# Level masks ahead of the inverse, keys times state ahead of the inverse: two edits to the gated DeltaNet of a two-layer encoder trunk

## The chip, the cores and the metric

One NeuronCore of a Trainium2 chip runs the whole program in one launch. The metric is the device time of one execution in microseconds (us). The engines are named as in the profile: PE (TensorE matmuls), PEld (its weight loads, which overlap PE), DVE (VectorE), ACT (ScalarE), POOL (GpSimd) and SP (SyncE, which issues most DMAs). PE's clock is granted at one of two levels, 1.2 and 2.4 GHz; a granted clock of 1.00 is the upper one, 0.50 the lower one.

## What is computed

The input is 512 tokens of 1024 channels, float32. Each of two layers is a half-step SwiGLU feed-forward, a token mixer, and another half-step feed-forward. In the mixer a combined projection feeds a gated DeltaNet branch (4 heads of 128) and a sliding-window attention branch. The part that the change touches is the gated delta rule:

```python
lower = jnp.where(strict, jnp.einsum('bnhid,bnhjd->bnhij', k_beta, kc) * decay, 0.0)
a_mat = jnp.eye(CHUNK) + lower
rhs = jnp.concatenate([v_beta, k_beta * jnp.exp(gc)[..., None]], axis=-1)
sol = triangular_solve(a_mat, rhs, left_side=True, lower=True, unit_diagonal=True)
u_c, w_c = sol[..., :dv], sol[..., dv:]
def step(state, inp):
    v_new = u_i - w_i @ state
    o = (q_i * exp(g_i)) @ state + a_i @ v_new
    state = state * exp(g_last) + (k_i * exp(g_last - g_i)).T @ v_new
```

So new values are A⁻¹ V − (A⁻¹ K) S, with A unit lower triangular, S the running state of a head and K the keys scaled by their decay.

## The kernel before, in words

PE's time goes into weight matmuls. Weights come from HBM in chunks of 128x1024; each is loaded by a DMA of SP into one of two raw buffers, copied by ACT to a rounded high part (line 911, `whi`), and the rest is made by DVE (line 1295, `wlo`): that pair is called the split of a chunk. PE multiplies each tile three times (lines 522 to 524: high by high, high by low, low by high). In the mixer, chunk j's 24 matmuls of 512 columns (12 for the half-size chunks 16 to 19) are followed by the list `MIX_STEPS[j]`, which is written out by hand in `mix_steps`. All five engines walk the same list in the same order, each doing its own part of every step; each engine is strictly in order, and the split of chunk j+3 is the first thing that ACT and DVE do in step list j. The steps hand PSUM banks 4 to 7 (and 2, 3) to each other through two counters per bank: `misc[b]` (PE has written it) and `misc_out[b]` (it has been read). `banks_of` says which bank a step uses; `count_uses` numbers the uses.

The steps that matter here, in the order of the list:

- `ktr` t: PE transposes the keys of token tile t; ACT squares them (line 1100, for the norm), DVE scales them twice, to `kte` (line 1584) and `ktl` (line 1585). `knorm` and `kk` then make the masked product matrix `NN`.
- SP takes the 16x16 diagonal blocks of `NN` out through HBM (`dg_home`, `tri`). `solve` (lines 1547 to 1557): DVE inverts them by a chain of 30 small, linked instructions. SP sends the result round through HBM again to `blk`, and `zb` (lines 1535 and 1542) makes from it Z, two halves of eight 64x64 inverses, and its transpose `Zt`.
- `invp` and `invd` i, lev: for each half i, two levels (4: 16 to 32, 5: 32 to 64) of doubling the inverted blocks. `invp` multiplies `Zt` by `Cs`, the part of `NN` that the level's mask keeps. `Cs` is made by POOL (line 1768) in the step itself, after POOL has seen both halves of Z; PE's part is line 721. ACT copies the product to `Pm` (line 1127), and `invd` (PE line 733, DVE line 1571) multiplies and subtracts. All of these are 64x64 matmuls of 32 columns.
- `vx`, `zx`, `zcp` complete the 128x128 inverse `Zf` from the halves.
- `wt` t (chunks 25 and 26): PE multiplies `kte` by `Zf` (line 779), ACT copies minus the product to `wneg` (line 1176).
- `sv` t (chunk 25+3t): PE accumulates `Zf` times values `vtm` (line 823) and, for t over 0, `wneg` times state S (line 825); DVE scales to `vn` (line 1621).
- `so` t (chunk 26+3t): PE makes the output and the state's update (lines 833, 841, 846), DVE makes S (lines 1628, 1633) and `o`.
- `vtr` t: transposes of the values (PE line 742, ACT line 1121). `qtr` t: transposes of the queries into bank 5 (PE line 698), squared by ACT (line 1111). `vwin`: transposes of the attention's values into bank 5, copied by ACT (lines 1167, 1168). `rope`, `swap`, `kmask` (ACT line 1149, which waits for the fifth `rope`): rotary positions. `sc`, `scn`, `pt`, `pv`: the windowed attention.

## Time and profile before

| | us |
|---|---|
| median of 3 runs | 2246.32 |
| lowest, highest of them | 2243.83, 2246.43 |
| profiled execution, its own time | 2241.95 |
| its span, first to last instruction | 2240.2 |
| PE busy in the span | 2212.7 (99%) |
| DVE, ACT, POOL busy | 1005.5, 845.0, 76.0 |
| mean granted clock of PE | 0.997 |

Times in the profile are counted from the span's start. The first mixer lies at about 390 to 760 us, the second at about 1500 to 1870 us. PE rows overlap (a matmul's row runs on while the next has begun), so what a group of matmuls costs is read from its start to the start of the next group. A float32 matmul is recorded as two rows, so the 16 matmuls of 128x128 in two `wt` steps and the like show twice their number.

### The profile page before, as it was taken

The numbers are of one execution on the slowest core, as the hardware profiler recorded it, in microseconds if no ns is written. First come the engines' busy times: TensorE is split into PE (matmuls) and PEld (weight loads), VectorE is DVE, ScalarE is ACT, GpSimd is POOL, SyncE is SP. The second block draws the span as 40 slices with busy tenths as digits, with TensorE's granted clock in tenths as the row PEclk, the third lists the DMA queues.
The fourth block names the chain that finished last, engine by engine and source line by source line (L and its number), as shares of the span: only waits on it lengthen the run. The fifth ranks groups of instructions, "written<-read, shape, count | busy, mean of one in ns | idle before, by whom it ended". The sixth has DMA issues, their size and how long they took to land. (4 is left out here: it accounts for less than half of the span.)

```text
span 2240.2 us, 29019 instructions
## 1 busy us (share of the span) xinstructions
PE 2212.7 (99%) x11356; PEld 1855.9 (83%) x11356; DVE 1005.5 (45%) x1422; ACT 845.0 (38%) x1499; POOL 76.0 (3%) x104
## 2 busy tenths in 40 slices
PE   7999999999999999999999999999999999999998
PEld 7888888888888888888888888887788888888887
DVE  4434324595536543442253433246944456344323
ACT  5323214655533532331252322156555335223211
POOL 0000000001000100000000000010100001000000
PEclk9999999999999999999999999999999999999999
DMA  4232222332123333222232232223312242332232
GB/s 164 94 99 96 96 97 82 124 91 67 57 76 124 107 107 99 97 94 96 84 113 94 94 103 94 95 84 123 92 57 66 84 142 89 101 102 94 94 100 79
DMA packets 71126, 215.83 MB, mean 96 GB/s; under 512 B 18928, under 2 KB 19440, under 8 KB 70256
## 3 DMA queue, kind: packets, MB, share of 16 engines
q1 hardware_dynamic: 69008, 201.82, 27.7%
q0 software_dynamic: 2016, 12.58, 1.5%
q8 instruction: 72, 1.18, 0.2%
q14 instruction: 30, 0.25, 0.0%
HBM read 206.77 MB, written 7.60 MB: 96 GB/s over the span
## 5 line engine op out<-in xcount | busy, mean ns | idle before, releaser
L1295 DVE TENSOR_TENSOR wlo<-raw,whi 128x1024 fp32r<-128x1024 f32 (+1 forms) x376 | 457.9, 1218 | 895.8 <-ACT whi L911 885.8
L522 PE MATMUL ps<-uhi,whi 128*128 128x512 f32 (+1 forms) x2208 | 829.8, 376 | 3.7 <-DVE wlo L1295 1.6
L523 PE MATMUL ps<-ulo,whi 128*128 128x512 f32 (+1 forms) x2208 | 821.5, 372 | 0.0
L524 PE MATMUL ps<-uhi,wlo 128*128 128x512 f32 (+1 forms) x2208 | 821.3, 372 | 0.0
L911 ACT ACTIVATE whi<-raw 128x1024 fp32r<-128x1024 f32 (+1 forms) x372 | 390.9, 1051 | 930.7 <-PE ps L524 547.2
L522 PEld LDWEIGHTS ps<-uhi,whi 128*128 128x128 f32 x2208 | 418.5, 190 | 78.3 <-issue 4.2
L524 PEld LDWEIGHTS ps<-uhi,wlo 128*128 128x128 f32 x2208 | 418.1, 189 | 72.2
L523 PEld LDWEIGHTS ps<-ulo,whi 128*128 128x128 f32 x2208 | 418.4, 189 | 69.8
L569 PE MATMUL ps<-whi,hhi 128*128 128x512 f32 x704 | 274.4, 390 | 0.0
L571 PE MATMUL ps<-whi,hlo 128*128 128x512 f32 x704 | 274.0, 389 | 0.0
L570 PE MATMUL ps<-wlo,hhi 128*128 128x512 f32 x704 | 273.9, 389 | 0.0
L571 PEld LDWEIGHTS ps<-whi,hlo 128*128 128x128 f32 x704 | 132.1, 188 | 27.6
L570 PEld LDWEIGHTS ps<-wlo,hhi 128*128 128x128 f32 x704 | 132.2, 188 | 27.2
L569 PEld LDWEIGHTS ps<-whi,hhi 128*128 128x128 f32 x704 | 132.2, 188 | 27.2
L998 ACT ACTIVATE tmp<-ps 128x512 f32<-128x512 f32 x88 | 52.8, 600 | 98.9 <-PE ps L524 98.4
L1376 DVE SCALAR_TENSOR_TENSOR tmp<-tmp,ps 128x512 f32<-128x512 f32 x88 | 60.2, 684 | 41.8 <-ACT tmp L998 41.8
L1001 ACT ACTIVATE hhi<-tmp 128x512 f32 (+1 forms) x88 | 55.5, 630 | 51.4 <-DVE tmp L1379 51.4
L1715 POOL TENSOR_TENSOR ry<-msy,neghalf 128x1 f32<-128x1 f32 x24 | 17.9, 744 | 1494.2 <-DVE msy L1302 1494.2
L1385 DVE SCALAR_TENSOR_TENSOR hlo<-tmp,hhi 128x512 f32 (+1 forms) x88 | 60.6, 689 | 12.0 <-ACT hhi L1001 10.8
L1379 DVE TENSOR_TENSOR tmp<-tmp,ps 128x512 f32<-128x512 f32 x88 | 60.5, 688 | 7.7
L1479 DVE SCALAR_TENSOR_TENSOR tmp<-cv,prm,tmp 128x512 f32<-128x512 f32 x72 | 54.0, 750 | 7.9 <-ACT tmp L1062 6.1
L1337 DVE SCALAR_TENSOR_TENSOR ulo<-ps,prm,uhi 128x256 fp32r<-128x256 f32 x96 | 42.2, 480 | 30.4 <-ACT uhi L961 30.4
(216 smaller groups left out, 1573.6 us busy)
## 6 DMA issues: line engine op xcount, KB each, us to landing
raw<-in_wstream_dram SPq DMA_DIRECT2D x368, 512.0 KB, 3.4
x_home<-x POOLq DMA_DIRECT2D x4, 1024.0 KB, 4.3
x<-x_home POOLq DMA_DIRECT2D x2, 2048.0 KB, 8.5
gain<-in_gp_dram POOLq DMA_DIRECT2D x6, 512.0 KB, 6.0
x<-in_x_dram SPq DMA_DIRECT2D x4, 512.0 KB, 7.8
raw<-in_wstream_dram SPq DMA_DIRECT2D x8, 256.0 KB, 3.7
out_dram<-x SPq DMA_DIRECT2D x8, 256.0 KB, 2.0
rcs<-in_rope_dram POOLq DMA_DIRECT2D x2, 512.0 KB, 4.1
```

Of the source, the lines that this page charges most:

```text
L522: pe.matmul(o, lh, bhi, start=first, stop=False)
L523: pe.matmul(o, lh, blo, start=False, stop=False)
L524: return pe.matmul(o, ll, bhi, start=False, stop=last)
L569: pe.matmul(o, shi[:, k, tok], whi[:, s, w], start=k == 0, stop=False)
L570: pe.matmul(o, shi[:, k, tok], wlo[:, s, w], start=False, stop=False)
L571: last = pe.matmul(o, slo[:, k, tok], whi[:, s, w], start=False, stop=k == kn - 1)
L911: act.activation(whi[:, s, 0:cols], raw[:, s % RAWS, 0:cols], ACT.Copy).then_inc(hi_done.h, 1)
L1001: act.activation(hhi[:, bass.ds(it * 2 + i, 1), :].rearrange("p a s -> p (a s)") if not isinstance(it, int) else hhi[:, 2 * it + i, :], tm ...
L1295: dve.tensor_tensor(wlo[:, s, 0:cols], raw[:, s % RAWS, 0:cols], whi[:, s, 0:cols].bitcast(f32), ALU.subtract) \
L1376: dve.scalar_tensor_tensor(tmp[:, i, :], tmp[:, 4 + i, :], 1.0, bank(4 * odd + 2 * i), ALU.add, ALU.mult).then_inc(tile_read.h, 1)
L1379: dve.tensor_tensor(tmp[:, 2 + i, :], tmp[:, i, :], bank(4 * odd + 2 * i + 1), ALU.mult).then_inc(tile_read.h, 1)
L1385: dve.scalar_tensor_tensor(lo, tmp[:, 2 + i, :], 0.5, hi.bitcast(f32), ALU.mult, ALU.subtract) \
```

## The change

It has four parts. (1) The masks `Cs` of level 4 are made by POOL in a new step `cmask` of list 14, as soon as DVE has finished `silu` 10, which is the instruction ahead of its `solve`; those of level 5 stay where they were. The two halves of `zb` are made one after the other (multiply, transpose, multiply, transpose). (2) `wt`, `kte` and `wneg` are gone. For t over 0 a new step `ks` in list 24+3t multiplies the keys by the state S ahead of the inverse, DVE scales it by the decay and subtracts the values from it into `vtm`, and `sv` has only the product by `Zf`, whose sign DVE turns while it scales. (3) The steps around the inverse are reordered: `vtr` 3 between the two `invp` of level 4, `qtr` 2 between the two `invd` of level 5, `qtr` 3 ahead of the evacuations of list 23, and `kmask` behind `vwin` 0 and `qtr` 0. (4) `qtr` squares into other buffers, which are free one `rope` earlier.

```diff
@@ mix_steps
-    s[14] = [("conv", 11), ("silu", 10), ("solve",)]
+    s[14] = [("conv", 11), ("silu", 10), ("solve",), ("cmask",)]
...
-    s[18] = [("qk", 0), ("qk", 1), ("rope", 2), ("rope", 3), ("vtr", 3)]
-    s[19] = [("evac", 16), ("evac", 17), ("swap", 4), ("invp", 0, 4), ("invp", 1, 4), ("rope", 4)]
-    s[20] = [("kmask",), ("vwin", 0), ("invd", 0, 4), ("qtr", 0), ("invd", 1, 4)]
+    s[18] = [("qk", 0), ("qk", 1), ("rope", 2), ("rope", 3)]
+    s[19] = [("evac", 16), ("evac", 17), ("swap", 4), ("invp", 0, 4), ("vtr", 3), ("invp", 1, 4), ("rope", 4)]
+    s[20] = [("vwin", 0), ("invd", 0, 4), ("qtr", 0), ("kmask",), ("invd", 1, 4)]
...
-    s[22].insert(0, ("qtr", 2))
-    s[23].insert(4, ("qtr", 3))
+    s[22].insert(1, ("qtr", 2))
+    s[23].insert(0, ("qtr", 3))
     s[24] = [("zx", 0), ("zx", 1), ("lq",)]
-    s[25] = [("qk", 3), ("wt", 0), ("wt", 1)]
-    s[26] = [("wt", 2), ("wt", 3)]
+    s[25] = [("qk", 3)]
+    s[26] = []
...
     for t in range(TT):
+        if t:
+            s[24 + 3 * t].append(("ks", t))
         s[25 + 3 * t].append(("sv", t))
@@ PE
-                    elif k == "wt":
-                        ...
-                            last = pe.matmul(bank(b, h * P, P), kte[:, t, h, :], Zf[:, 4 * t + h, :], start=True, stop=True)
+                    elif k == "ks":
+                        t = step[1]
+                        use(L, step, 4)
+                        pe.wait_ge(s_new.h, s_new.at(L, t))
+                        free_of_waits()
+                        for h in range(H):
+                            last = pe.matmul(bank(4, h * P, P), kq[:, 0, h, P * t:P * t + P], S[:, h, :], start=True, stop=True)
+                        done(last, 4)
...
                         if t:
-                            got(("wt", t), banks_of(("wt", t))[0])
-                            pe.wait_ge(s_new.h, s_new.at(L, t))
+                            got(("ks", t), 4)
...
                         for h in range(H):
-                            last = pe.matmul(bank(4, h * P, P), Zf[:, 4 * t + h, :], vtm[:, t, h, :], start=True, stop=t == 0)
-                            if t:
-                                last = pe.matmul(bank(4, h * P, P), wneg[:, h, P * t:P * t + P], S[:, h, :], start=False, stop=True)
+                            last = pe.matmul(bank(4, h * P, P), Zf[:, 4 * t + h, :], vtm[:, t, h, :], start=True, stop=True)
@@ ACT
                         if t == 0:
-                            act.wait_ge(roped.h, roped.at(L, 5))
+                            act.wait_ge(roped.h, roped.at(L, 4))
...
-                            last = act.activation(tmp[:, 2 + t % 2, h * P:(h + 1) * P], bank(5, h * P, P), ACT.Square,
+                            last = act.activation(tmp[:, 4 + t % 2, h * P:(h + 1) * P], bank(5, h * P, P), ACT.Square,
...
-                    elif k == "wt":
-                        ...
@@ DVE
-                        for i in range(2):
-                            s8 = slice(8 * i, 8 * i + 8)
                             dve.wait_ge(z1_done.h, z1_done.at(L, i + 1))
                             dve.transpose(Zt[:, s8, :].rearrange("p c j -> p (c j)"), Z[:, s8, :].rearrange("p c j -> p (c j)")) \
...
-                        dve.tensor_tensor(kte[:, t, :, :], src, cols(exs, 4 * t, 4, P), ALU.mult)
...
-                        dve.tensor_tensor(vn[:, :, :], bank(4).rearrange("p (h d) -> p h d", d=P), cols(wcol, 4 * t, 4, P), ALU.mult) \
+                        dve.scalar_tensor_tensor(vn[:, :, :], bank(4).rearrange("p (h d) -> p h d", d=P), -1.0 if t else 1.0,
+                                                 cols(wcol, 4 * t, 4, P), ALU.mult, ALU.mult).then_inc(misc_out[4].h, 1)
+                    elif k == "ks":
+                        t = step[1]
+                        ready(step, 4)
+                        got(("vtr", t), banks_of(("vtr", t))[0])
+                        for h in range(H):
+                            last = dve.scalar_tensor_tensor(vtm[:, t, h, :], bank(4, h * P, P), exs[:, 4 * t + h:4 * t + h + 1], vtm[:, t, h, :],
+                                                            ALU.mult, ALU.subtract)
+                        last.then_inc(misc_out[4].h, 1)
@@ POOL
+                def level_mask(i, lev):
+                    s8 = slice(8 * i, 8 * i + 8)
+                    pool.tensor_tensor(Cs[:, s8, :], NN[:, s8, 0:CH], many(con[:, K_LEV + 64 * (lev - LEVELS[0]):][:, 0:64], 8),
+                                       ALU.mult).then_inc(c_done.h, 1)
...
+                    elif k == "cmask":
+                        pool.wait_ge(silu_done.h, silu_done.at(L, 11))
+                        for i in range(2):
+                            level_mask(i, LEVELS[0])
...
-                        pool.tensor_tensor(Cs[:, s8, :], NN[:, s8, 0:CH], many(con[:, K_LEV + 64 * (lev - LEVELS[0]):][:, 0:64], 8),
-                                           ALU.mult).then_inc(c_done.h, 1)
-                        if lev > LEVELS[0]:
+                            level_mask(i, lev)
```

## Rows read from the trace of the kernel before

**Rows 1.** Page, part 1: busy us, share, instructions of each engine.
```profile
PE 2212.7 (99%) x11356; PEld 1855.9 (83%) x11356; DVE 1005.5 (45%) x1422; ACT 845.0 (38%) x1499; POOL 76.0 (3%) x104
```

**Rows 2.** Waits of PE: us in total, times, longest.
```profile
PE ps L698 <- ACT vwin L1168: 3.5, 2, 2.6
...
PE ps L721 <- issue: 0.9, 2, 0.6
```

**Rows 3.** Timeline of PE, chunks 25 and 26: start, us, idle before.
```profile
562.20 1.95 PE L779 MATMUL ps<-Zf,kte 128*128 128x128 f32 x16
564.08 0.66 PE L809 MATMUL ps<-pT,vwin 64*64 64x128 f32 x8
...
566.03 1.05 PE L823 MATMUL ps<-vtm,Zf 128*128 128x128 f32 x8
566.84 0.48 PE L522 MATMUL ps<-uhi,whi 128*128 128x512 f32 x1
```

**Rows 4.** Timeline of PE, `sv` 1 of the first mixer.
```profile
593.22 0.38 PE L823 MATMUL ps<-vtm,Zf 128*128 128x128 f32 x2
...
594.92 0.48 PE L522 MATMUL ps<-uhi,whi 128*128 128x512 f32 x1
```

**Rows 5.** Groups by line, DVE.
```profile
L1584 DVE TENSOR_TENSOR kte<-ps,exs 128x512 f32<-128x512 f32 x8 | 5.5, 684 | 0.0
```

**Rows 6.** Timeline of DVE around the end of list 27.
```profile
587.09 0.15 DVE L1648 SCALAR_TENSOR_TENSOR mo<-sso,eqs 128x4 f32<-128x4 f32 x1
...
605.94 1.12 DVE L1633 SCALAR_TENSOR_TENSOR S<-S,exs,ps 128x128 f32<-128x128 f32 x4 [1.25 <-PE ps L846]
```

**Rows 7.** Timeline of PE, second mixer, list 20.
```profile
1624.63 0.66 PE L698 MATMUL ps<-con,kq 128*128 128x128 f32 x4 [2.57 <-ACT vwin L1168]
```

**Rows 8.** Timeline of PE, first mixer, chunk 18 and list 19.
```profile
494.67 0.48 PE L522 MATMUL ps<-uhi,whi 128*128 128x512 f32 x1
...
503.18 1.12 PE L721 MATMUL ps<-Zt,Cs 64*64 64x32 f32 x32 [0.53 <-POOL Cs L1768]
504.87 1.12 PE L721 MATMUL ps<-Zt,Cs 64*64 64x32 f32 x32 [0.57 <-issue]
506.31 0.52 PE L522 MATMUL ps<-uhi,whi 128*128 128x512 f32 x1 [0.32 <-ACT sk L1055]
```

**Rows 9.** Timeline of POOL and DVE, first mixer, list 19.
```profile
503.51 1.26 POOL L1768 TENSOR_TENSOR Cs<-NN,con 128x512 f32<-128x512 f32 x1
...
503.74 2.12 DVE L1295 TENSOR_TENSOR wlo<-raw,whi 128x1024 fp32r<-128x1024 f32 x1 [0.81 <-ACT whi L911]
```

**Rows 10.** Timeline of DVE, first mixer: the solve and what follows.
```profile
486.39 0.17 DVE L1551 TENSOR_TENSOR prod<-tri,sol 128x15 f32<-128x15 f32 x1
...
493.50 0.69 DVE L1295 TENSOR_TENSOR wlo<-raw,whi 128x512 fp32r<-128x512 f32 x1
...
499.28 1.23 DVE L1295 TENSOR_TENSOR wlo<-raw,whi 128x1024 fp32r<-128x1024 f32 x1
500.42 1.29 DVE L1535 TENSOR_TENSOR Z<-blk,con 128x512 f32<-128x512 f32 x2
501.62 1.30 DVE L1542 STREAM_TRANSPOSE Zt<-Z 128x512 f32<-128x512 f32 x2
```

**Rows 11.** Second mixer: DVE's split of chunk 18, PE's start on it.
```profile
1602.18 0.69 DVE L1295 TENSOR_TENSOR wlo<-raw,whi 128x512 fp32r<-128x512 f32 x1
...
1604.07 0.48 PE L522 MATMUL ps<-uhi,whi 128*128 128x512 f32 x1
```

**Rows 12.** Windows: us, busy (x) of PE, PEld, DVE, ACT, POOL, granted clock, DMA.
```profile
506.00:510.00 4.00, 3.69 (x9) 2.94 (x10) 3.97 (x7) 3.07 (x7) 1.00 (x1) 0.57 0.40 133
533.00:538.00 5.00, 5.00 (x104) 4.79 (x103) 1.23 (x4) 1.14 (x8) 0.00 (x0) 0.93 0.35 108
538.00:541.00 3.00, 3.00 (x10) 2.48 (x10) 1.17 (x5) 1.38 (x10) 0.95 (x1) 0.55 0.00 0
...
1626.00:1629.00 3.00, 3.00 (x18) 2.40 (x15) 2.36 (x3) 1.53 (x5) 0.53 (x1) 0.53 0.18 72
```

More of the change, by code:

```diff
@@ L161, in banks_of @@
         return ((7, 4) if x == 0 else (6, 7))[:1 if step[2] == LEVELS[0] else 2]
-    if k == "wt":
-        return (7,) if x % 2 == 0 else (4,)
     if k == "pt":
@@ L261, in trunk @@
         kq = at("kq", [P, 2, H, SEQ], 0)
-        wneg = at("wneg", [P, H, SEQ], 0)
         vT = at("vT", [P, H, SEQ], 16 * kb)
@@ L280, in trunk @@
         Zt = at("Zt", [P, 16, CH], 68 * kb)
-        kte = at("kte", [P, TT, H, P], 72 * kb)
         cv = at("cv", [P, 4, 516], 80 * kb)
@@ L1172, in do @@
                                            ACT.Copy).then_inc(misc_out[5].h, 1)
-                    elif k == "wt":
-                        t, b = step[1], banks_of(step)[0]
-                        ready(step, b)
-                        act.activation(wneg[:, :, t * P:(t + 1) * P], bank(b).rearrange("p (h c) -> p h c", c=P), ACT.Copy,
-                                       scale=-1.0).then_inc(misc_out[b].h, 1)
                     elif k == "sc":
@@ L1538, in do @@
                                .then_inc(z1_done.h, 1)
-                        for i in range(2):
-                            s8 = slice(8 * i, 8 * i + 8)
                             dve.wait_ge(z1_done.h, z1_done.at(L, i + 1))
```

14 lines of the change are left out of this document (5 added, 9 removed).

## The prediction, as it was put on record before the run

> **What bounds the kernel now.** I read the page first. PE is busy 99% of the span and DVE and ACT under half [rows 1], so a change is worth what it does to PE's line of work: matmuls taken off it, and waits of PE that end or begin. Shorter work elsewhere counts only where PE waits for it. So the second view is PE's own waits. In the mixers they are few: 3.5 us in two waits of `qtr` 0 for ACT's copy of `vwin` (line 1168), and about 1.4 us of `invp` (line 721) for POOL's masks, 0.9 put down to "issue" [rows 2] and 0.5 to POOL [rows 8]. The third is the timeline of PE and DVE through lists 14 to 26, where the change lies, and the fourth the granted clock in windows there, because the timeline shows chunks that run slow behind the small matmuls.
>
> **`wt` gone.** From the start of `wt` 0 to the start of what follows it is 564.08 - 562.20 = 1.88 us for two steps [rows 3]. There are two such pairs in a mixer and two mixers: 4 x 1.88 = 7.5 us of PE's time, with nothing beside it.  ACT's four copies to `wneg` go too, and were hidden.
>
> **`sv` and `ks`.** `sv` 1 with both products takes 594.92 - 593.22 = 1.70 us [rows 4]. After, `sv` is like `sv` 0, 566.84 - 566.03 = 0.81 us [rows 3], and `ks` has the same four matmuls, 0.81 to 0.9. The sum is the same as before. What is added is one more place where PE changes from weight matmuls to a step, six times; the first matmul behind a step is longer than the others (0.48 us in [rows 3]), so I allow 0.07 us each, an estimate, +0.4 us in all (bounds 0 and +0.6).
>
> **Does PE wait for `ks`?** `ks` t needs S from the list before, and `sv` t needs DVE's result one chunk after `ks`. DVE's part is four scalar_tensor_tensor of 128x128 from PSUM, which is the form of line 1633: 1.12 us for four [rows 6]. In front of it in DVE's queue are the softmax's four small instructions and `on`, whose end is at 587.24 [rows 6]. So DVE is done near 588.5, and PE asks for it at about 593.2, when `sv` 1 stood before [rows 4]. The cover is over 4 us; the cost is 0. What queues behind DVE's wait in that list is `zsilu` and the split of chunk 31, three chunks ahead of PE; both wait for ACT anyway. If that cover were gone, every microsecond of lateness would cost six.
>
> **`kmask` behind `qtr`.** In list 20 ACT waits for the fifth `rope` before it may copy `vwin` 0, and PE stands behind bank 5: 2.57 us in the second mixer, the rest of the 3.5 in the first [rows 2, 7]. After, ACT reads bank 5 as soon as PE has written it, and PE has `invd` 0 in between, 32 small matmuls like those of line 721, 1.12 us [rows 8], longer than ACT's copy. DVE's own lateness there is met by a chunk of cover before `invp` of level 5. I take all of it: -3.5 us (bounds -3.5 and -2.5, if DVE's later `zt` should reach PE).
>
> **Masks early: the gain and its price.** The gain is bounded by the 1.4 us [rows 2, 8]. In the first mixer `invp` 0 starts at 503.18 after 0.53 us and `invp` 1 after 0.57 [rows 8]; `Zt` is the next to be late, and it was there at 502.9 at the latest [rows 10].
>
> The price is in the place where the masks go. `cmask` is released by the same instruction of DVE behind which `solve` begins, at 486.39 [rows 10], and POOL reaches for the memory together with a chain of 30 linked DVE instructions. The trace shows what POOL's mask does to a DVE instruction that reads two SBUF tensors: the split that starts at 503.74, with POOL's `Cs` running from 503.51 to 504.77, takes 2.12 us [rows 9], and the one at 499.28, of the same shape, 1.23 [rows 10]. That is a hold until POOL's instruction has ended. No row shows it for the solve's small ones, so I bound: the hold is between 0 and 2 x 1.26 = 2.5 us a mixer, and I take 2.5, by the nearest row. From it goes what DVE no longer does: 4 x 0.6 us for `kte` (0.684 as recorded, 0.6 from start to start) [rows 5]. Of these 2.4 us about half is lost again, since the second `ktl` must wait for ACT's squares; I follow DVE's continuous row of work from `ktr` to `kk` 3 and get 1.15 us. So the solve ends about 2.5 - 1.15 = 1.35 us later (bounds -1.15 and +2.5).
>
> What is late next: the first thing behind the solve is the split of chunk 18, done at 494.19 where PE starts on chunk 18 at 494.67 [rows 8, 10]: only 0.48 us of cover, less 0.1 for the handover, so PE waits about 0.95 us. In the second mixer the cover is 1604.07 - 1602.87 = 1.20 [rows 11], and PE waits 0.25. The result's two DMAs, `zb`, the next load and ACT's evacuations behind it all move by the same 1.35. `invp` 0 then finds `Zt` at about the time it comes, and chunk 20 waits for ACT's evacuation of `sk`, as it did before by 0.32 [rows 8], now some 0.65 later, as ACT no longer has `vtr` 3 in front. Chunk 20 starts at about 507.0 for 506.31, and 0.6 late in the second mixer. So the masks' gain and price together are +1.2 us; with no hold they are -1.4, with the full hold and nothing from `kte` +3.7.
>
> The Trainium skill's page "GPSIMD Engine Reference" (section "Key points") says that POOL shares its SBUF interfaces with VectorE and contends with DVE instructions that have two SBUF inputs; by it the solve, all of whose instructions have two, is held as the split was, and the sum is the one I take; were the rule not to reach them, the sum would be that of the second rival. The rule speaks against this change, and the row of the split agrees with it, 2.12 us for 1.23.
>
> **The clock.** Three stretches of the mixers ran at half the clock: 0.57 over 506 to 510, 0.55 over 538 to 541 with 0.93 before it [rows 12], and 0.53 over 1626 to 1629 [rows 12]. Each costs (1 - 0.57) x 4 = 1.7 us, or (1 - 0.55) x 3 + (1 - 0.93) x 5 = 1.7. Before each, PE had 3 to 4 us of nothing but 64x64 matmuls of 32 columns and waits. Two of the three had a wait in them that the change ends or shortens, and the third was two `invd` and their double products back to back (104 matmul rows in 533 to 538). After, `vtr` 3, `qtr` 0 and `qtr` 2 (128x128, 128 columns) stand between them. The second mixer has no fall at the place of the third, so it is not certain even before. I take 2.4 of the three falls as gone: -4.0 us (bounds 0 and -5.1). An early stall of 0.9 us at chunk 18 does not stand beside small matmuls.
>
> **The rest.** `qtr` 3 ahead of the evacuations delays ACT by 1.8 us into list 24; I find `zx` still covered by 0.4 us or more. `vn` as scalar_tensor_tensor reads and writes the same elements, and DVE is far from the bound there. Both 0.
>
> **Sum.** -7.5 + 0.4 - 3.5 + 1.2 - 4.0 = -13.4 us. On the profiled execution that is 2241.95 - 13.4 = 2228.5, its span 2226.8. The three timed runs stand 1.9 to 4.5 us above that execution, for no reason that the profile shows; I carry the difference over to the median: 2246.3 - 13.4 = 2232.9 us, -0.6%.
>
> **Rivals.**
> - *The full hold and a clock that still falls.* POOL's masks cost 2.5 us a mixer with no relief, and the new stall and the still small matmuls keep the falls: -7.5 + 0.6 - 3.5 + 3.7 = -6.7, 2239.6 us. For it: the cover of 0.48 us. Against: the waits inside the small stretches do shrink. 0.2.
> - *No hold.* The solve's instructions slip between POOL's, the masks' waits are gone: -7.5 - 3.5 - 1.4 - 5.1 = -17.5, 2228.8 us. For it: no row of a small instruction held. Against: the row of the split. 0.2.
> - *Nothing is left.* The freed PE time turns into waits for something else, the weights' loads first: within 4.5 us of before. For it only that the chunks 16 to 20 are already near their loads; against, the rest of the mixer has splits three chunks ahead. 0.05.
> - *Slower: `ks` is not covered.* If DVE's part of `ks` came after `sv`'s place, PE would stand six times. To end 4.5 us over before, it has to eat 13.4 + 4.5 = 17.9 us, 3.0 us each: DVE would have to end 7 us later than the 588.5 above, behind the next splits. That gives 2251 us. Its point of decision is the end of DVE's fourth instruction against PE's `sv`. 0.03.
>
> **How the numbers follow.** The forecast has 0.5 (its own range 2230 to 2236, from the 1.2 and the 4.0 each going half-way to their bounds), the rivals 0.48, and 0.02 is for more than all of it. 0.2% of 2246 is 4.5 us, about what a measurement of this kernel can tell from no change. The range of 8 in 10 reaches from the second rival to the first and takes in a spread of the runs of about 1.5 us on the lower side: 2227 to 2240. Faster 0.91, same 0.05, slower 0.04.
>
> **What would show it.** No rows of lines 779 and 1176, a `ks` line with 48 rows on PE, `sv` with 64. POOL's `Cs` of level 4 inside the solve, with two instructions of lines 1551 and 1553 of over 1 us instead of 0.2: the hold. PE idle before chunk 18 of the first mixer for about 1 us behind `wlo`, less in the second. No wait of `qtr` behind `vwin`. `sv` without a wait for `vtm`. Windows of half clock in the mixers: none or one for three. The prediction is wrong if the solve ends more than 2.5 us later, if PE waits at `zx` or `sv`, or if the clock falls as often as before.

## The result, and the profile after

The changed kernel takes 2229.73 us (median of 5, 2228.74 to 2229.96). The kernel before has a median of 2243.83 over five runs (2239.06 to 2246.43), of which three are those of the table above and two are new. The ratio is 0.9941, 95% interval 0.9929 to 0.9953: 0.6% faster. The profiled execution took 2229.16, its span 2227.4, which is 12.8 us less than the span before.

The page's part 1 shows PE 12.9 us less busy than in [rows 1], with 64 rows fewer, which are the 32 matmuls of `wt`, each recorded as two rows.

```profile
PE 2199.8 (99%) x11292; PEld 1842.5 (83%) x11292; DVE 1013.8 (46%) x1438; ACT 841.5 (38%) x1491; POOL 74.7 (3%) x104
```

PE's waits after the change, to be read against [rows 2] (us in total, times, longest):

```profile
PE ps L783 <- DVE attnT L1519: 2.6, 2, 1.3
...
PE ps L520 <- ACT sk L1050: 1.7, 2, 0.8
...
PE ps L719 <- DVE Zt L1530: 0.5, 2, 0.3
```

The 3.5 us of `qtr` behind `vwin` are gone. New, and not forecast, is `sc` 3 (line 783) behind `attnT`, DVE's multiply of `qk` 3: 1.3 us in each mixer.

DVE's timeline where the solve begins in the first mixer, and the split of chunk 18 behind it, against [rows 10]:

```profile
483.73 0.17 DVE L1539 TENSOR_TENSOR prod<-tri,sol 128x15 f32<-128x15 f32 x1
483.94 1.29 DVE L1541 TENSOR_TENSOR sol<-sol,prod 128x15 f32<-128x15 f32 x1
485.26 1.22 DVE L1539 TENSOR_TENSOR prod<-tri,sol 128x28 f32<-128x28 f32 x1
486.51 0.19 DVE L1541 TENSOR_TENSOR sol<-sol,prod 128x28 f32<-128x28 f32 x1
...
492.97 0.69 DVE L1285 TENSOR_TENSOR wlo<-raw,whi 128x512 fp32r<-128x512 f32 x1
```

And POOL's timeline at the same place:

```profile
483.89 2.54 POOL L1738 TENSOR_TENSOR Cs<-NN,con 128x512 f32<-128x512 f32 x2 [26.91 <-DVE kq L1482]
```

Two instructions of the solve take 1.29 and 1.22 us while POOL makes its two masks, where 0.17 to 0.20 is usual: a hold of 1.1 + 1.05 = 2.15 us. Measured from PE's first transpose of v, at 490.68 before and 489.65 after, the solve starts 1.63 us sooner, and the split of chunk 18 comes 0.50 later. The second mixer shows the change alone: there the solve starts 1.01 us sooner (at 1595.07 with the transpose at 1600.08 before, at 1586.73 with 1592.75 after), and the split of chunk 18 comes 1.14 later than in [rows 11]. About 0.5 of the first mixer's 1.63 is no part of the change: `order_alone` and `masks_alone` (below), which still have `kte`, start the solve 0.49 and 0.44 us sooner than before there, and within 0.1 us of before in the second mixer. In the trace of before, ACT's split ahead of the solve waited 2.64 us for a late load, and DVE stood 0.87 us for ACT. The two rows are ACT's of before and DVE's of the changed kernel:

```profile
482.26 0.64 ACT L911 ACTIVATE whi<-raw 128x512 fp32r<-128x512 f32 x1 [2.64 <-DMA raw<-in_wstream_dram]
```
```profile
1595.99 0.69 DVE L1285 TENSOR_TENSOR wlo<-raw,whi 128x512 fp32r<-128x512 f32 x1
```

PE's timeline at chunk 18, list 19, `qtr` 0 and list 25 of the first mixer, against [rows 3, 8]:

```profile
493.71 0.50 PE L520 MATMUL ps<-uhi,whi 128*128 128x512 f32 x1
...
501.50 1.12 PE L719 MATMUL ps<-Zt,Cs 64*64 64x32 f32 x32 [0.26 <-DVE Zt L1530]
...
505.08 0.47 PE L520 MATMUL ps<-uhi,whi 128*128 128x512 f32 x1 [0.81 <-ACT sk L1050]
...
512.23 0.66 PE L696 MATMUL ps<-con,kq 128*128 128x128 f32 x4
...
557.68 0.66 PE L794 MATMUL ps<-con,pexp 128*128 128x128 f32 x4
559.67 1.10 PE L783 MATMUL ps<-skz,sq 128*128 128x256 f32 x4 [1.33 <-DVE attnT L1519]
560.61 1.05 PE L820 MATMUL ps<-vtm,Zf 128*128 128x128 f32 x8
```

No row of PE shows a wait at chunk 18, but the split ends only 0.05 us ahead of it in the first mixer (493.66 for 493.71) and 0.06 in the second (1596.68 for 1596.74). `qtr` 0 starts without idle time. `sc` 3 is what PE now waits for.

The clock, in windows from the first transpose of v to `vx` in each mixer, the stretch in which the windows of [rows 12] lie:

```profile
489.65:540.29 50.64, 49.57 (x490) 41.70 (x488) 36.74 (x64) 26.74 (x76) 5.76 (x7) 1.00 0.30 90
1592.75:1643.34 50.59, 49.50 (x489) 41.69 (x488) 36.76 (x63) 26.75 (x76) 5.71 (x7) 1.00 0.30 90
```

The granted clock is 1.00 in both: none of the three falls to the 1.2 GHz level is left. This is no accident of one execution: the mean granted clock over the whole span is on record for every timed run, and it is 0.999 in all five of the changed kernel and all five of `changed_again` (below), while 42 of the 44 timed runs of before that have one lie between 0.995 and 0.998 (one has 0.993, one 0.999).

To compare the kernels, PE's line of work is cut at the same steps in each. Stretch A goes from the first v transpose to `vx`, stretch B from `vx` to the first transpose of `o`. The rest of the two mixers is equal to 0.1 us in all kernels (except in `qk3_late`, told below). The clock is the mean granted clock in A. All times are from the profiled execution of each; the last columns are timed runs.

| kernel | A, mixer 1 (clock) | A, mixer 2 (clock) | B, mixers 1, 2 | span | median (low to high) | ratio to before, interval |
|---|---|---|---|---|---|---|
| before | 54.75 (0.94) | 53.94 (0.97) | 57.09, 57.09 | 2240.2 | 2243.83 (2239.06 to 2246.43) | |
| changed | 50.64 (1.00) | 50.59 (1.00) | 55.00, 55.00 | 2227.4 | 2229.73 (2228.74 to 2229.96) | 0.9941, 0.9929 to 0.9953 |
| `changed_again` | 50.69 (1.00) | 50.58 (1.00) | 54.98, 54.99 | 2227.7 | 2230.03 (2229.48 to 2231.62) | 0.9951, 0.9938 to 0.9965 |
| `keys_alone` | 53.06 (0.97) | 55.98 (0.91) | 53.69, 53.69 | 2233.2 | 2235.28 (2232.73 to 2237.39) | 0.9973, 0.9962 to 0.9985 |
| `order_alone` | 50.05 (1.00) | 49.74 (1.00) | 57.04, 57.04 | 2229.9 | 2232.72 (2231.64 to 2235.61) | 0.9965, 0.9951 to 0.9978 |
| `masks_alone` | 54.84 (0.94) | 54.88 (0.94) | 57.08, 57.08 | 2240.0 | 2244.47 (2241.33 to 2248.94) | 1.0016, 1.0007 to 1.0025 |
| `qk3_late` | 52.34 (0.97) | 50.45 (1.00) | 52.58, 52.58 | 2225.5 | 2227.3 (2226.3 to 2228.0) | 0.9935, 0.9922 to 0.9949 |
| `qtr3_back` | 50.64 (1.00) | 50.55 (1.00) | 53.70, 53.71 | 2224.7 | 2228.24 (2226.48 to 2228.63) | 0.9941, 0.9927 to 0.9955 |
| `masks_back` | 49.33 (1.00) | 49.33 (1.00) | 54.98, 54.98 | 2224.5 | 2226.81 (2226.25 to 2228.08) | 0.9937, 0.9923 to 0.9950 |
| `masks_twice` | 52.55 (1.00) | 52.78 (1.00) | 54.99, 54.98 | 2231.6 | 2234.26 (2233.38 to 2236.15) | 0.9970, 0.9957 to 0.9982 |
| `kmask_back` | 56.27 (0.94) | 58.49 (0.91) | 53.70, 53.73 | 2238.3 | 2239.43 (2237.27 to 2241.73) | 0.9990, 0.9981 to 0.9998 |
| `slices_back` | 56.08 (0.94) | 52.68 (0.97) | 53.72, 53.71 | 2232.3 | 2231.84 (2229.48 to 2234.07) | 0.9954, 0.9940 to 0.9969 |
| `masks_13` | 51.73 (0.97) | 50.05 (1.00) | 55.01, 54.99 | 2227.7 | 2228.69 (2228.25 to 2229.91) | 0.9943, 0.9929 to 0.9956 |
| `both_back` | 49.33 (1.00) | 49.33 (1.00) | 53.72, 53.69 | 2221.9 | 2224.14 (2223.2 to 2224.5) | 0.9922, 0.9908 to 0.9935 |

`changed_again` is the changed kernel once more, on the chip of the kernels that it is compared with. Three sets shared a chip and the runs of before: `keys_alone`, `order_alone`, `masks_alone`, `qk3_late` (before 2240.95); `changed_again`, `qtr3_back`, `masks_back`, `masks_twice` (before 2241.76); and `kmask_back`, `slices_back`, `masks_13`, `both_back` (before 2241.34).

### The profile page after: what moved, and what is told of

The parts are those of the page before. It is cut to its first block and busy times, and to the rows that moved or that the text cites. A ratio compares the mean times of both kernels' runs of the same rounds, so it can differ in the third digit from the quotient of the medians.

```text
span 2227.4 us, 28889 instructions
## 1 busy us (share of the span) xinstructions
PE 2199.8 (99%) x11292; PEld 1842.5 (83%) x11292; DVE 1013.8 (46%) x1438; ACT 841.5 (38%) x1491; POOL 74.7 (3%) x104
```

## The experiments

**One part of the change at a time.** Three kernels are the kernel before with one part of the change each. `keys_alone`:

```diff
-    s[25] = [("qk", 3), ("wt", 0), ("wt", 1)]
-    s[26] = [("wt", 2), ("wt", 3)]
+    s[25] = [("qk", 3)]
+    s[26] = []
+        if t:
+            s[24 + 3 * t].append(("ks", t))
...
-                        dve.tensor_tensor(kte[:, t, :, :], src, cols(exs, 4 * t, 4, P), ALU.mult)
```

> The kernel before with ks in the place of wt and without kte and wneg; masks, v slice 3, the q squares' place and kmask as before. Theory from the two traces: the 64 matmuls of wt (7.5 us) go, but the 1.88 us of wt 0 and wt 1 had hidden what sc 3 waits for (bank 5, which DVE's multiply of qk 3 frees), so a wait of about 1.3 us a mixer stands in front of sc 3 (2.6), and the sum is -4.7 with the clock unchanged: about 2239 against 2244. kte's relief of DVE (0.6 a mixer) reaches a little of the stalls at chunks 18 to 20, -0.5 at most. Rival 1, nothing is exposed: -7.1. Rival 2, what the removal does to the clock: each fall of the clock inside a mixer that is gone gives 1.6 to 1.7 more, each new one takes as much, and the windows with a granted clock under 0.9 show which.

Measured: 0.9973, 5.7 us under before. B is 3.40 shorter in each mixer, 6.8 in all: `wt`'s 7.5 less 0.7, which I put down to the `ks` and `sv` steps standing apart (it is the remainder, not a row). The expected wait of `sc` 3 is not there; nothing stands between `pt` 1 and `sc` 3 but `pt`'s own 0.64 us, and PE's timeline has no idle time before it:

```profile
560.77 0.66 PE L794 MATMUL ps<-con,pexp 128*128 128x128 f32 x4
561.41 1.10 PE L783 MATMUL ps<-skz,sq 128*128 128x256 f32 x4
```

So the removal of `wt` alone does not expose the wait; the theory I had from the two traces was wrong. ACT's timeline of this kernel in list 23 shows what differs. It evacuates z at once and squares `qtr` 3 (line 1106) behind that:

```profile
541.29 2.31 ACT L1050 ACTIVATE z<-ps 128x512 f32<-128x512 f32 x4
543.50 0.27 ACT L1106 ACTIVATE tmp<-ps 128x128 f32<-128x128 f32 x1
```

In the changed kernel ACT comes to `qtr` 3 first and stands 2.02 us until PE has made the transposes:

```profile
540.39 0.28 ACT L1106 ACTIVATE tmp<-ps 128x128 f32<-128x128 f32 x1 [2.02 <-PE ps L696]
...
541.66 2.07 ACT L1050 ACTIVATE z<-ps 128x512 f32<-128x512 f32 x4
```

DVE's multiply of `qk` 3 follows from it. In `keys_alone` it starts 1.38 us behind PE's `qk` 3, which PE began at 559.20, and in the changed kernel 2.73 us behind it, begun at 556.11. The two rows of DVE, `keys_alone` first:

```profile
560.58 0.68 DVE L1519 TENSOR_TENSOR attnT<-attnT,ps 128x512 f32<-128x512 f32 x1
```
```profile
558.84 0.68 DVE L1519 TENSOR_TENSOR attnT<-attnT,ps 128x512 f32<-128x512 f32 x1
```

The clock moved as well: 0.97 and 0.91 for 0.94 and 0.97. The falls cost (1 - 0.97) x 53.06 + (1 - 0.91) x 55.98 = 6.6 us, where those of before cost (1 - 0.94) x 54.75 + (1 - 0.97) x 53.94 = 4.9. And this kernel, which makes the masks where before made them, has no wait of `invp` for them in either mixer: with `kte` gone they are there in time.

`order_alone` (its list edits; with them `qtr`'s squares go to `tmp` 4 and 5 and wait for four `rope`s in place of five):

```diff
-    s[18] = [("qk", 0), ("qk", 1), ("rope", 2), ("rope", 3), ("vtr", 3)]
-    s[19] = [("evac", 16), ("evac", 17), ("swap", 4), ("invp", 0, 4), ("invp", 1, 4), ("rope", 4)]
-    s[20] = [("kmask",), ("vwin", 0), ("invd", 0, 4), ("qtr", 0), ("invd", 1, 4)]
+    s[18] = [("qk", 0), ("qk", 1), ("rope", 2), ("rope", 3)]
+    s[19] = [("evac", 16), ("evac", 17), ("swap", 4), ("invp", 0, 4), ("vtr", 3), ("invp", 1, 4), ("rope", 4)]
+    s[20] = [("vwin", 0), ("invd", 0, 4), ("qtr", 0), ("kmask",), ("invd", 1, 4)]
-    s[22].insert(0, ("qtr", 2))
-    s[23].insert(4, ("qtr", 3))
+    s[22].insert(1, ("qtr", 2))
+    s[23].insert(0, ("qtr", 3))
```

> The kernel before with the reordering alone: v slice 3 between invp 0 and invp 1, kmask behind q square 0, the squares' scratch tiles, q squares 2 and 3 each a step earlier; wt, kte and masks as before. Theory from the two traces: the wait of q square 0 behind vwin's copy goes (3.5 us over both mixers), and nothing else is lost: -3.5. If the falls of the clock come from the small matmuls that stand together at chunks 18 to 20 and 22 to 24, they are gone here too and the time is 5 lower still, -8.5; if wt was the cause of a fall, they stay and it is -3.5. Rival: invp 0 comes 0.6 us sooner and waits for its masks and for Zt that much longer (0.6 a mixer, 1.2), which leaves -2.3.

Measured: 0.9965, 8.2 us under before. A is 4.69 and 4.20 shorter, 8.9 in all, and the windows show a full clock:

```profile
489.61:539.67 50.06, 49.51 (x490) 41.71 (x488) 35.83 (x60) 26.71 (x76) 8.57 (x9) 1.00 0.29 91
1594.13:1643.87 49.74, 49.48 (x489) 41.70 (x487) 35.62 (x59) 26.74 (x76) 8.55 (x9) 1.00 0.31 91
```

Of the 8.9, the falls were 4.9 and the waits 4.0. So the reordering can take all three falls away without `wt` or the masks being touched. (The profiled execution, 2231.64, is the fastest of this kernel's five. The slowest, 2235.61, has a mean clock of 0.999 over its span like the profiled one; two falls more would show in that number, so falls do not account for the 4.0 us between them.) `invp` still waits 0.9 us in all for POOL's masks, so `vtr` 3 between the two `invp` does not end that wait by itself. Here PE still has `wt` 0 and 1 (1.88 us) between `qk` 3 and `sc` 3, and B is unchanged: ACT's lateness is covered by them.

`masks_alone` (`cmask` beside the solve, `zb`'s halves one after the other, all else as before):

```diff
-    s[14] = [("conv", 11), ("silu", 10), ("solve",)]
+    s[14] = [("conv", 11), ("silu", 10), ("solve",), ("cmask",)]
```

> The kernel before with the masks alone: the level 4 masks on POOL while DVE runs the substitution, and zb's two halves each with its transpose. Theory: POOL's two masks hold DVE by about 1.1 us each (2.15 a mixer), the solve ends 2.15 later than before (there is no relief of kte here), the split of chunk 18 is that late and PE stands at chunk 18 for 1 to 2 us; the waits for Cs (0.53 a mixer) go, part of the lateness falls into chunk 20's own waits. Sum +1 to +3 over both mixers. Rival 1, PE has enough in front of it that the hold is paid by nobody: -0.5 to -1.4. Rival 2, the clock: a stall longer than before moves a fall, +-1.7 each.

Measured: 1.0016, 3.5 us over before, a little more than expected. The profiled execution is not the place to read it: at 2241.80 it lies at the low end of runs from 2241.33 to 2248.94, and its span is that of before. It does show the kind: the waits of PE at chunks' starts grow (wlo 3.7 us for 1.6, sk 3.3 for 0.6), while the 3.5 of `qtr` 0 behind `vwin` is gone. That PE has lost that time earlier fits both, but was not tested.

```profile
PE ps L522 <- DVE wlo L1295: 3.7, 8, 1.0
PE ps L522 <- ACT sk L1055: 3.3, 2, 1.7
```

**Where the wait of `sc` 3 comes from.** `qk3_late` is the changed kernel with the step that holds bank 5 taken away from there:

```diff
-    s[25] = [("qk", 3)]
+    s[25] = []
+    s[30].append(("qk", 3))
```

> The changed kernel with qk 3 taken out of list 25 and put at the end of list 30, where bank 5 has been read for the last time and so 3 (list 35) is still five chunks away. Theory: sc 3 waits in the changed kernel for bank 5, which DVE's multiply of qk 3 frees (1.3 us a mixer), so this gives 2.6 us over the changed kernel: about 2227, and the wait row of sc 3 behind DVE attnT is gone. Rival: sc 3 then waits for the exponentials of sc 2 or for another of DVE's jobs of the same stretch, and the wait only changes its name: within 0.5 us of the changed kernel. Second rival: the multiply, now in list 30, holds a step of the state chain there: slower by up to 1.3 in place of faster.

Measured: 0.9935. Against `changed_again` B is 2.40 shorter in each mixer, and the stretch up to the last transpose of `o`, which now holds `qk` 3, is 1.02 longer in the first mixer and 0.90 in the second: 1.4 and 1.5 us net, for the 1.3 expected. The row of `sc` 3 behind `attnT` is gone. It gives 2.9 in the trace, of which a fall of the clock in the first mixer (0.97) takes back 1.6. The cause of the wait was then tested at the other end, in `qtr3_back`, the changed kernel with one number changed:

```diff
-    s[23].insert(0, ("qtr", 3))
+    s[23].insert(4, ("qtr", 3))
```

> The changed kernel with q square 3 back behind the four evacuations of list 23, where it stood before; all else as changed. Theory: in the changed kernel ACT reaches the squares of q square 3 first, waits there 2.02 us for PE's transposes and evacuates only then, so its split of chunk 28, and with it DVE's multiply of qk 3, come 1.4 us later against PE than with the keys alone; so the wait of sc 3 (1.3 us a mixer) comes from this move and goes with it: 2.6 under the changed kernel, and no wait row of sc 3 behind DVE attnT. Rival 1: PE has moved ahead of the whole DVE queue by the 3.5 us that the reordering gave it, whatever ACT does, and the wait stays: within 0.5 of the changed kernel. Rival 2: vx waits for the later evacuations, which takes it back.

Measured: B is 1.28 shorter in each mixer, 2.6 in all, A and the clock are unchanged, and the wait is gone. ACT evacuates 3.3 us sooner than in the changed kernel, and PE goes from `pt` 1 to `sc` 3 without a stop:

```profile
538.36 2.31 ACT L1050 ACTIVATE z<-ps 128x512 f32<-128x512 f32 x4
```
```profile
557.84 0.66 PE L794 MATMUL ps<-con,pexp 128*128 128x128 f32 x4
558.47 1.10 PE L783 MATMUL ps<-skz,sq 128*128 128x256 f32 x4
```

By the timed runs it is 1.8 us under `changed_again`, on medians with ranges of 2.1 us each. So the chain is: PE's `qtr` 3, ACT's wait of 2.0, ACT's later split, DVE's later multiply of `qk` 3, bank 5, `sc` 3. PE itself makes the same steps in the same order in both kernels.

**What the masks cost.** `masks_back` is the changed kernel with level 4's masks in `invp` and `zb` as before:

```diff
-    s[14] = [("conv", 11), ("silu", 10), ("solve",), ("cmask",)]
+    s[14] = [("conv", 11), ("silu", 10), ("solve",)]
```

> The changed kernel with the masks as before (level 4 in invp, both of zb's products ahead of the transposes); keys and reordering as changed. Theory: the reordering alone against the changed kernel puts the masks at +0.6 and +0.85 us from the first v transpose to vx, so without them it is 1.4 under the changed kernel: about 2228.3; DVE's substitution runs from its start to its end in 9.3 less 2.15 us, and a wait for Cs of about 0.6 stands at invp 0 again. Rival 1: the wait for Cs is worth as much as the hold: within 0.5. Rival 2: without the stall at chunk 20 or with the one at invp 0 a fall of the clock comes back: 1.7 slower for each.

Measured: 0.9937, 3.2 us under `changed_again` on the same chip. A is 1.36 and 1.25 shorter: 2.6 us, about twice what I expected. PE is busy for all of the 49.33 us of A in both mixers: no wait for `Cs`, for `Zt` or for `sk` is left. DVE's timeline has the solve from 483.45 to the split at 490.55, 7.10 us, where the changed kernel takes 9.24:

```profile
483.45 0.17 DVE L1541 TENSOR_TENSOR prod<-tri,sol 128x15 f32<-128x15 f32 x1
...
490.55 0.68 DVE L1285 TENSOR_TENSOR wlo<-raw,whi 128x512 fp32r<-128x512 f32 x1
```
```profile
489.45:538.78 49.33, 49.33 (x490) 41.64 (x488) 33.72 (x55) 26.67 (x76) 9.02 (x9) 1.00 0.31 92
```

`masks_twice` doubles the suspected cost:

```diff
                         for i in range(2):
+                            pool.tensor_tensor(Cs[:, 8 * i:8 * i + 8, :], NN[:, 8 * i:8 * i + 8, 0:CH],
+                                               many(con[:, K_LEV:][:, 0:64], 8), ALU.mult).then_inc(pool_link.h, 1)
+                            pool.wait_ge(pool_link.h, pool_link.at(L, 2 + i))
                             level_mask(i, LEVELS[0])
```

> The changed kernel with each of the two level 4 masks made twice by POOL, one product behind the other, so that POOL runs four products of 1.27 us beside the substitution in place of two. Theory: while POOL's product runs, DVE's instruction does not end, so four instructions of the substitution take 1.2 to 1.3 us in place of 0.2, the solve ends 2.15 later than in the changed kernel, and since DVE has next to nothing to spare up to chunk 18, PE pays 1.5 to 2.1 of it in each mixer: +3 to +4.3 against the changed kernel. Rival 1: the hold is a single one at the start of POOL's work, not one for each product: below +0.5. Rival 2: the hold is there, but waits that stand there anyway (0.8 at chunk 20, 0.26 at invp 0) take it up: +1 to +2.

Measured: 4.2 us over `changed_again`, A longer by 1.86 and 2.20. Four instructions of POOL, four long ones of DVE; each is held until POOL's has ended. POOL's and DVE's timelines:

```profile
484.07 1.30 POOL L1762 TENSOR_TENSOR Cs<-NN,con 128x512 f32<-128x512 f32 x1 [26.84 <-DVE kq L1482]
485.45 1.34 POOL L1738 TENSOR_TENSOR Cs<-NN,con 128x512 f32<-128x512 f32 x1
```
```profile
484.11 1.30 DVE L1541 TENSOR_TENSOR sol<-sol,prod 128x15 f32<-128x15 f32 x1
485.45 0.19 DVE L1539 TENSOR_TENSOR prod<-tri,sol 128x28 f32<-128x28 f32 x1
485.67 1.17 DVE L1541 TENSOR_TENSOR sol<-sol,prod 128x28 f32<-128x28 f32 x1
486.88 1.23 DVE L1539 TENSOR_TENSOR prod<-tri,sol 128x39 f32<-128x39 f32 x1
488.14 1.35 DVE L1541 TENSOR_TENSOR sol<-sol,prod 128x39 f32<-128x39 f32 x1
```

The wait of PE for `wlo` grows from 1.6 to 5.4 us, which is the price at the chunk behind the solve. PE stands 1.9 us there in each mixer, behind the 512-column matmuls of a chunk and one step of transposes, and the granted clock of A stays at 1.00.

Which instructions of DVE are held can be read from before's own masks, which run beside others. After the split of [rows 9] DVE's next two rows, whose inputs are one tile in SBUF and one in PSUM (`ps`), take 0.65 us each beside POOL's second mask, no more than the 0.68 of one elsewhere. POOL's row, which starts while the split still runs, takes 1.80 in place of 1.28:

```profile
505.20 1.80 POOL L1768 TENSOR_TENSOR Cs<-NN,con 128x512 f32<-128x512 f32 x1
```
```profile
505.88 1.29 DVE L1529 TENSOR_TENSOR attnT<-attnT,ps 128x512 f32<-128x512 f32 x2
```
 `masks_13` moves the masks beside longer instructions with two inputs in SBUF:

```diff
-    s[13] = [("conv", 10), ("silu", 9)]
-    s[14] = [("conv", 11), ("silu", 10), ("solve",), ("cmask",)]
+    s[13] = [("cmask",), ("conv", 10), ("silu", 9)]
+    s[14] = [("conv", 11), ("silu", 10), ("solve",)]
```

> The changed kernel with POOL's two level 4 masks moved from the substitution to list 13, beside DVE's convolution, where DVE's instructions are 0.7 to 0.8 us long and DVE has 0.61 and 0.25 us of idle time before the solve. Theory: POOL's product holds DVE wherever DVE works, long instructions as well (2.15 us in all), but 0.86 of it falls into the idle time there: the solve starts 1.3 later and takes 2.15 less, 0.4 to 0.9 a mixer under the changed kernel, 0.8 to 1.7 in both. Rival 1: long instructions are not held, and it is worth the whole of masks_back, 2.6 under. Rival 2: the idle time there is not real slack, since ACT's chain moves with DVE: within 0.4 of the changed kernel.

Measured: 0.9943, as good as the changed kernel. In the second mixer A is 0.53 shorter than in `changed_again`, as expected; in the first it is 1.04 longer, with a clock of 0.97, which is (1 - 0.97) x 51.73 = 1.6 us, so 0.5 shorter but for the fall. The hold has moved with the masks, to a split and to the convolution's three instructions together, 1.37 for 0.69 and 3.36 for 2.33:

```profile
476.33 1.37 DVE L1285 TENSOR_TENSOR wlo<-raw,whi 128x512 fp32r<-128x512 f32 x1 [0.57 <-ACT whi L906]
477.62 3.36 DVE L1469 SCALAR_TENSOR_TENSOR tmp<-cv,prm,tmp 128x512 f32<-128x512 f32 x3
```

**What brings the clock down.** Two kernels undo one part of the reordering each, and are read against `qtr3_back`. `kmask_back`:

```diff
-    s[20] = [("vwin", 0), ("invd", 0, 4), ("qtr", 0), ("kmask",), ("invd", 1, 4)]
+    s[20] = [("kmask",), ("vwin", 0), ("invd", 0, 4), ("qtr", 0), ("invd", 1, 4)]
-    s[23].insert(0, ("qtr", 3))
+    s[23].insert(4, ("qtr", 3))
-                            act.wait_ge(roped.h, roped.at(L, 4))
+                            act.wait_ge(roped.h, roped.at(L, 5))
```

> The changed kernel with q square 3 behind the evacuations (as in qtr3_back, the comparison for this one) and kmask back at the head of list 20, with the squares' scratch tiles and their wait for roped as before; v slice 3 and q square 2 stay where the change put them. Theory: ACT's copy of vwin 0 comes behind kmask again and PE stands at q square 0 for 1.75 to 2.6 us a mixer: +3.5 to +5.1 over qtr3_back. On the clock, theory A: PE's standing still there is what brings the falls inside the mixers, so one to three come back at 1.7 each: +5 to +10 in all. Theory B: it is the small matmuls that stand together in front of chunks 20 and 22, which this kernel still has spread: no fall, +3.5 to +5.1.

Measured: A longer by 5.63 and 7.94 us, 13.6 in all, more than either theory allowed; the timed median is 11.2 higher (on another chip). PE's waits and the windows:

```profile
PE ps L696 <- ACT vwin L1163: 6.3, 2, 3.2
```
```profile
489.77:546.04 56.27, 52.08 (x490) 43.61 (x488) 36.90 (x64) 28.53 (x80) 5.82 (x7) 0.94 0.26 81
1597.12:1655.61 58.49, 54.26 (x490) 45.41 (x488) 36.58 (x64) 28.63 (x80) 5.93 (x7) 0.91 0.27 83
```

The wait is 6.3 us, where before had 3.5 and `keys_alone` 5.1; DVE's `rope` behind the held solve may be what makes it longer, which no run here tests. The falls cost (1 - 0.94) x 56.27 + (1 - 0.91) x 58.49 = 8.6. The two together are 14.9, against 13.6: the two overlap in part, and where PE stands anyway a fall costs nothing. Not all of the falls belong to the wait. One in the second mixer begins at the end of list 22, where `qtr` 2 stands between the small matmuls as in the changed kernel and PE has no wait:

```profile
1642.00:1647.00 5.00, 5.00 (x99) 4.36 (x98) 0.81 (x3) 1.14 (x8) 0.00 (x0) 1.00 0.30 105
1647.00:1650.50 3.50, 3.50 (x18) 3.05 (x18) 1.66 (x6) 0.64 (x5) 0.95 (x1) 0.54 0.02 5
```

`slices_back`:

```diff
-    s[18] = [("qk", 0), ("qk", 1), ("rope", 2), ("rope", 3)]
-    s[19] = [("evac", 16), ("evac", 17), ("swap", 4), ("invp", 0, 4), ("vtr", 3), ("invp", 1, 4), ("rope", 4)]
+    s[18] = [("qk", 0), ("qk", 1), ("rope", 2), ("rope", 3), ("vtr", 3)]
+    s[19] = [("evac", 16), ("evac", 17), ("swap", 4), ("invp", 0, 4), ("invp", 1, 4), ("rope", 4)]
-    s[22].insert(1, ("qtr", 2))
-    s[23].insert(0, ("qtr", 3))
+    s[22].insert(0, ("qtr", 2))
+    s[23].insert(4, ("qtr", 3))
```

> The changed kernel with q square 3 behind the evacuations (as in qtr3_back, the comparison for this one), v slice 3 back in list 18 and q square 2 back at the head of list 22; kmask stays behind q square 0. No work is added and no wait is known of. Theory A on the clock (the wait at q square 0 brings the falls): no fall inside a mixer, within 0.6 of qtr3_back in the trace; invp 0 and invp 1 run without the 0.58 of v slice 3 between them, so a wait for the second half's Zt of up to 0.7 a mixer can show: +0 to +1.4. Theory B (small matmuls standing together): one to three falls come back at 1.7 each: +1.7 to +5.

Measured: median 3.6 us over `qtr3_back` (on another chip; the profiled execution, 2234.07, is the slowest of six). The falls are back with no wait at `qtr` 0 at all:

```profile
489.53:545.60 56.07, 52.46 (x489) 44.01 (x487) 37.57 (x71) 28.48 (x80) 5.40 (x7) 0.94 0.29 88
1596.88:1649.60 52.72, 50.89 (x491) 42.91 (x489) 36.09 (x64) 28.34 (x80) 5.41 (x7) 0.97 0.29 86
```

(The second window ends 0.04 us behind `vx`.) The second mixer has no late load in it: +2.13, of which the fall is 1.6. But another wait has grown. Without `vtr` 3 between the two `invp`, PE stands 1.76 us in the second mixer and 1.75 in the first for ACT's evacuation of `sk`, where `qtr3_back` has 0.73 and 0.74:

```profile
PE ps L520 <- ACT sk L1050: 3.5, 2, 1.8
```

The fall of the second mixer begins at the end of that wait, at about 1613, and the first of the two in the first mixer within it, at about 507. The third, at 538.0, follows 4.5 us from 533.0 in which PE was busy throughout with `qtr` 2 and the two `invd`, back to back. In the first mixer, +5.44, another thing came on top in this execution: a load of weights landed late, ACT's split behind it started at 481.27 for 478.70 in `qtr3_back`, and the `silu` of DVE that stands ahead of the solve at 484.80 for 483.23:

```profile
481.27 0.64 ACT L906 ACTIVATE whi<-raw 128x512 fp32r<-128x512 f32 x1 [3.60 <-DMA raw<-in_wstream_dram]
```

So theory A (only the wait at `qtr` 0 brings the falls) is out, and theory B (only the small matmuls that stand together) is out by `kmask_back`, where they are spread and falls come. What `slices_back` does not separate, at chunk 20, is the small matmuls standing together from the 1.75 us wait behind them; only its fall in list 22 came without a wait beside it, as that of [rows 12] at 537 did. `qk3_late` and `masks_13` show one fall each in the first mixer, with the lists 15 to 24 as in the changed kernel: the reordering takes most of the falls away, but not so surely that every later edit is safe.

**The version without the two costs.** `both_back` has the edits of `masks_back` and `qtr3_back` together.

> The changed kernel without the two parts that the runs so far show to cost: masks as before, and q square 3 behind the evacuations; ks in the place of wt, v slice 3, q square 2 and kmask as changed. Theory: the two act in different stretches (v transposes to vx, and vx to the first output transpose) and add up: 2.6 and 2.6 under the changed kernel, 2224.5 by the trace, a ratio to before of 0.992. Rival 1: with the masks gone PE is ahead by 1.3 a mixer more and the wait of sc 3 comes back in part: 2.6 to 4 under. Rival 2: a fall of the clock comes back: 1.7 for each.

Measured: 2224.14 us (2223.2 to 2224.5), 0.9922, interval 0.9908 to 0.9935. The parts add up: A shorter by 1.36 and 1.25, B by 1.26 and 1.30 than `changed_again`. It is the fastest kernel of this study, 17.2 us under before, and by the spans 2227.7 - 2221.9 = 5.8 us under the changed one. The only wait of PE that its trace shows inside the two stretches is that of `sc` behind ACT's queue:

```profile
PE ps L783 <- ACTq L1110: 0.7, 2, 0.3
```

## Why the prediction was right, and where its steps were not

The forecast was -13.4 us on the profiled span; it moved by -12.8. The main terms were right in kind and size, but that the sum comes within 0.6 us is partly luck: a cost of 2.6 us that the forecast had at nothing was met by 0.5 more from the waits, 0.9 more from the clock, and 1.2 outside the stretches, most of which has nothing to do with the change. Step by step:

| step | forecast | measured | read from |
|---|---|---|---|
| `wt` gone, `ks` and `sv` apart | -7.1 | -6.8 | B of `keys_alone` |
| `qtr` 3 ahead of the evacuations | 0 | +2.6 | B of the changed kernel against `keys_alone` and `qtr3_back` |
| `kmask` behind `qtr` | -3.5 | -4.0 | A of `order_alone`, less the falls; 0.5 of it is `invp`'s shorter wait for the masks |
| masks, with `kte` gone | +1.2 | +1.4 | A of the changed kernel less A of `order_alone`: 101.23 - 99.79 |
| clock | -4.0 | -4.9 | A and clock of before and `order_alone` |
| outside the two stretches | 0 | -1.2 | span, of which 1.04 lies ahead of the first mixer |
| sum | -13.4 | -12.9 | |

- **The 1.04 us ahead of the first mixer** is no part of the change: in `changed_again` the same point is 0.4 later than in the changed kernel, in `keys_alone` it is 0.4 under before, in `masks_alone` 0.97.
- **`wt`, `ks`, `sv`.** The removal was as forecast. Taking `ks` and `sv` apart costs 0.35 us a mixer, in place of 0.2. That DVE is done long before `sv` asks is right: in the first mixer its four instructions start at 579.96 and take 1.12, and `sv` 1 starts at 586.89 without idle time.
- **The step that failed is "`qtr` 3 ahead of the evacuations ... I find `zx` still covered".** `zx` was covered. What was not covered was one link further, in the order of ACT's queue: the split, DVE's queue behind it, and bank 5. I looked only at the next user of what ACT delays. Nor did I ask what stood between `qk` 3 and `sc` 3 once `wt` was gone: the 1.88 us whose removal I had counted as gain were at the same time the cover for this. `order_alone` has the move, `keys_alone` has the removal, and neither waits; only both together do.
- **The hold.** Forecast 2.5 us a mixer, measured 2.15, in two instructions of 1.29 and 1.22 us as described. The relief from `kte` was about the 1.15 forecast: 1.01 in the second mixer, and in the first 1.14 against `order_alone`, which still has `kte` and starts its solve 4.78 us ahead of the first transpose of v, for 5.92 in the changed kernel. So the solve ended 1.0 to 1.1 later, for 1.35. Yet the waits of 0.95 and 0.25 at chunk 18 did not come. In the first mixer the cover of 0.48 us had been read from an execution in which DVE was about 0.5 late for a load; in the second the lateness of 1.14 just fitted into the cover of 1.20. That no wait shows is thus a matter of 0.05 us. What came in its place is at chunk 20: the wait for ACT's evacuation of `sk` is 0.81 for 0.32 in the first mixer and 0.85 for 0.30 in the second, and `Zt` costs 0.26 and 0.24. The term's size, 1.4 for 1.2, was right, and its parts are these: `masks_back` puts the masks at +2.6, and `kte` then stands at 1.4 - 2.6 = -1.2.
- **The gain of the masks** was bounded at 1.4 and is nothing. Once `kte` is out of DVE's queue, `Cs` is there in time without the early step: `keys_alone` and `masks_back` have no wait for it, while `order_alone`, which has `kte` and v slice 3 between the two `invp`, still waits 0.9. The waits of [rows 2, 8] came from a late DVE.
- **The Trainium skill**, page "GPSIMD Engine Reference", section "Key points", says that POOL and VectorE share SBUF interfaces and contend where a DVE instruction has two SBUF inputs. The rows agree, for the solve's instructions (1.29 for 0.18), for the split (1.37 for 0.69) and for the convolution (3.36 for 2.33 in three), and the multiply with one input in PSUM, which was not held (0.65 each), fits it too.
- **The clock.** That most of the falls go was right, and that they come back without `vtr` 3 and `qtr` 2 between the small matmuls is shown by `slices_back`; that they come with a longer wait at `qtr` 0 is shown by `kmask_back`. I had 2.4 of three, all three went. The prediction's "nothing but 64x64 matmuls of 32 columns and waits" does not hold for the second mixer: `qtr` 0, of 128x128, stood at 1624.63 between the wait and the fall at 1626.
- **The absolute time.** 2229.73 lies 3.2 under the 2232.9 forecast, while the ratio, 0.9941, is the forecast's 0.9940. I had carried over that the timed runs of before stood 4.4 above its profiled one; for the changed kernel that distance is 0.6, and the median of before itself fell to 2243.83 with two more runs and to 2240.95 to 2241.76 in the later sets. Against those, `changed_again` is 11.7 us under before, a little less than the 12.8 of the spans. The spread of the timed runs shrank from 7.4 us for before to 1.2. Falls of the clock that differ in number from one execution to the next explain part of this: the mean clocks on record differ by about 0.0025 between before and the changed kernel, which is 5.6 us of 2240, near the 4.9 of the traces, and the slowest run of before, 2249.33, has the lowest clock, 0.993. They do not explain all of it: `masks_alone` took 2241.33 at a mean clock of 0.996 and 2246.67 at 0.998.

Open is what exactly decides whether a fall comes. Neither the wait at `qtr` 0 nor the bunched small matmuls were needed, and two kernels with neither had one.

## What to carry to other kernels

When work is taken off the bounding engine, ask for each piece whether another engine's lateness was hiding behind it, and follow the queues to their next three users, not to the next one. Two edits that are harmless one by one can expose a wait together, so after a change with several parts it pays to run each part alone and to undo each alone: here two pieces cost 2.6 us each and were carried by the rest. Before a helper engine's work is moved "out of the way", look whose memory reads it runs beside: a wait that it was meant to end may end by itself once the busy engine has less to do.
